# A decoder block with expert retrieval: the second token tile's top-k moved partly into its own rows, thinner top-k pieces beside block 1's attention, and the first tile's final norm later

## The chip, the cores and the metric

The kernel runs on one core of one Trainium2 chip. The metric is the device time of one execution in microseconds (us). The engines are PE (TensorE, matmuls), DVE (VectorE), ACT (ScalarE), POOL (GpSimd) and SP (SyncE); each runs its own instruction stream in order, and the streams meet only in semaphores. Sixteen DMA engines move data for all of them.

## The reference, cut to what matters

The input is 1024 tokens of width 1024, float32. A mixer is followed by an expert retrieval layer (PEER) and a final norm:

```
h   = x + mixer(rmsnorm(x))            # stick-breaking attention (8 heads x 64) + mLSTM (4 heads x 128), gated, w_out
hn  = rmsnorm(h)
q   = hn @ w_query                     # 8 retrieval heads, two halves each
s1, s2 = scores of the halves against 128 keys each
v1, i1 = top_k(s1, 16);  v2, i2 = top_k(s2, 16)
top_s, top_c = top_k(v1[:, None] + v2[None, :], 16)         # of 256 candidates
e_idx = i1[top_c // 16] * 128 + i2[top_c % 16];  gate = softmax(top_s)
y   = h + sum over 8 heads x 16 experts of gate * gelu(u[e_idx] . hn) * v[e_idx]
out = rmsnorm(y)
```

Each token has experts of its own, so 128 rows of u and v (8 KB together) are fetched per token: 1.07 GB in all.

## The kernel before

**Two streams of work.** The 1024 tokens are 8 tiles (`TT`) of 128, and 4 blocks (`NB`) of two tiles. The mixer and the query scores run by block (`mix(b)` on each engine), the expert rows by tile. Block 0's mixer runs first and alone, up to its first queries (`N_HEAD` steps). After that a loop `for i in range(TT): for p in range(PP)` goes over 64 *pairs* of expert rows per tile, and every engine works in each pair on the tile's rows and then on some steps of a later block's mixer. A *slot* is one pair counted over all tiles: slot 64 is pair 0 of tile 1.

**One pair on each engine.** POOL gathers a row pair for 128 tokens (L926; 128 rows of 8 KB for each of the two) into `rowsb`, a ring of `RS = 8` rows (4 pairs); it waits for `v_done` before it overwrites a place, and for `experts_ready` before each 32 rows. DVE makes the two dot products (`dot`, L1629) and writes `dots`. ACT applies gelu (L1190), multiplies by the gate (L1202) and builds two diagonal matrices (`spread`, L1207). PE adds the two rows through them (`add_rows`, L856, 16 matmuls) into `yacc` and gives the ring's places back. After that each engine does its mixer steps of this slot.

**Order of the mixer steps.** `spread_ticks` places block b's steps on slots with estimated costs per engine (`slot_load`, `load_of`); the list `steps[slot][b]` is the same for all engines. A step with much work is followed by the next only in the next slot. For block 1 the slots 8 to 99 are used: attention steps (`sba`) in slots 22 to 29, the convolutions and the mLSTM projections (`PROJ2`) in 30 to 42, heads, gates and merge (`N_MIX`) in 43 to 73, then `w_out`, the norm and the queries to slot 99. Weights come in units of 512 KB on SP's queue into a ring of `WR = 3`: a unit's place is filled again once PE has used it.

**Top-k.** `top_parts(i, first, 2)` does the top-k of two retrieval heads (a *group*) of tile i on DVE, in 9 pieces (`TOP_EACH`), each ending in a `yield`. The last one raises `experts_ready`. A tile has 4 groups, 36 pieces. `parts_at[i][p]` says how many pieces pair p of tile i does; they stand between the dots and the mixer steps on DVE. In tile 0 they are the three remaining groups of tile 0 itself (its first group runs before the loop) and all four of tile 1, 63 pieces: none in pairs 0 and 1, then one per pair, two in pairs 44, 48, 52, 56 and 60. In tile 1 they are those of tile 2, from pair 26 on. Pieces 1 to 4 work on 128x128 scores (`max`, `max_index`, `match_replace`), 5 to 7 on 128x256 candidates, 8 and 9 on 128x512 (`eq`) in `wide`, the memory of `sc`.

**Gates.** After a group's last piece ACT takes exp of its scores (`gates`, L1185) and DVE makes the softmax (L1614 to L1618). Tile 0 does it by group in pairs 1, 11, 20 and 29 (`GATES_AT`); tile 1 and later ones once, at pair 62 of the tile before. `load_scores(1, g)` on ACT loads tile 1's scores of group g into `sc` at pairs 12, 13, 21 and 30 of tile 0 (`SCORES_AT`).

**End of a tile.** At pair 0 of the next tile DVE adds `yacc` to the residual (`residual`); ACT squares it at pair 3 into the tensor `wide`, which is the same memory as `sc` (`norm`, L1212); DVE scales at pair 5 (`final_norm`, L1651); ACT stores at pair 7 and loads the next residual at pair 20.

Of the kernel before, what the change touches and what calls it, by code (L numbers as in the profile page):

```python
# [19 lines left out]
TT = T // P  # L20
# [24 lines left out]
NT = 2  # L45
# [20 lines left out]
def build(nc, xT, x, vecs, w_feat, w_if, w_tok, w_merge, w_out, w_query, keysT, uv, rows, out):  # L66
    ctx = ExitStack()
    with ctx:
# [316 lines left out]

        cost = [load_of(b) for b in range(NB)]
        TOP_EACH, BLOCK_END = 9, 36
        GATES_AT, SCORES_AT = (1, 11, 20, 29), (12, 13, 21, 30)
        GATES_OF = ((1, 1), (2, 2), (4, 2), (6, 2))
        N_SLOT = TT * PP  # L390
        N_PARTS = 4 * TOP_EACH


        parts_at = [[0] * PP for i in range(TT)]
        for p in range(PP):
            parts_at[0][p] = 0 if p < 2 else 2 if p >= 44 and p % 4 == 0 else 1
            for i in range(1, TT - 1):
                if i % NT == 1:
                    due = p - 25 if p < BLOCK_END else 10 + (p - BLOCK_END + 1) * 13 // 8
                else:  # L400
                    due = (p - 15) * N_PARTS // 42
                parts_at[i][p] = max(0, min(due, N_PARTS)) - sum(parts_at[i][:p])


        def slot_load(s):
            i, p = divmod(s, PP)
            dve_ = 2.6 + PART_DVE * parts_at[i][p]
            if p == 0 and i > 0:
                dve_ += 4.5
            if p == 5 and i > 0:  # L410
                dve_ += 1.5
            return [2.6, dve_, 5.1]

        def spread_ticks(b, lo, hi, each):
            count, placed, k, behind = [0] * N_SLOT, [0] * N_SLOT, 0, [0.0] * 3
            for s in range(lo, hi):
                even = max(behind) <= 0.0
                behind = [max(0.0, q) + r - e for q, r, e in zip(behind, slot_load(s), (min(each, 6.4), each, each))]
                while k < len(cost[b]):
                    small = max(cost[b][k][:2]) < 0.9  # L420
                    if count[s] == (2 if b == 1 else 1) and not small:
                        break
                    after = [q + r for q, r in zip(behind, cost[b][k])]
                    if max(after) > 2.0 and not (even and count[s] == 0):
                        break
                    behind = after
                    count[s] += not small
                    placed[s] += 1
                    k += 1
            return placed, k  # L430
# [5 lines left out]
        for b in range(1, NB):  # L436
            lo = 8 if b == 1 else NT * (b - 1) * PP - PP + BLOCK_END
            hi = NT * b * PP - PP + BLOCK_END
            each = 5.0
            while spread_ticks(b, lo, hi, each)[1] < len(cost[b]):  # L440
                each += 0.02
            slot_of = []
            for s, n in enumerate(spread_ticks(b, lo, hi, each)[0]):
                steps[s][b] = n
                slot_of += [s] * n
            first = len(cost[b]) - N_QRY
            assert slot_of[first + 5] > (NT * b - 1) * PP + 3
            for g in range(4):
                assert sum(parts_at[NT * b - 1][:slot_of[first + 4 * g + 5] % PP + 1]) <= TOP_EACH * g


        with nc.Block() as block:
# [479 lines left out]
            def _(act):  # L932
# [246 lines left out]
                def gates(i, first, count):  # L1179
                    own = slice(TOPK * first, TOPK * (first + count))  # L1180
                    if (i, first) == (0, 0):
                        act.wait_ge(first_ready, 1)
                    else:
                        act.wait_ge(experts_ready, 4 * i + (first + count) // 2)
                    act.activation(gate[:, i % 2, own], gate_raw[:, own], ACT.Exp).then_inc(gexp_done, 1)  # L1185
# [6 lines left out]
                def spread(i, p):  # L1192
                    if i == 0 and p % 16 == 0:
                        act.wait_ge(gate_step, 3 * (p // 16) + (6 if p > 0 else 3))
                    elif i == 0 and p == 8:
                        act.wait_ge(gate_step, 6)
                    elif p == 0:
                        act.wait_ge(gate_step, 3 * i + 15)
                    act.wait_ge(gelu_done, i * PP + p + 1)
                    for k in (2 * p, 2 * p + 1):  # L1200
                        s = k % RS
                        act.activation(wg[:, s:s + 1], gmt[:, s:s + 1], ACT.Copy,  # L1202
                                       scale=gate[:, i % 2, k:k + 1]).then_inc(wg_done, 1)
                    act.wait_ge(wg_done, i * NSEL + 2 * p + 2)
                    for k in (2 * p, 2 * p + 1):
                        s = k % RS
                        last = act.activation(diag[:, s, :], ident7[:, :], ACT.Copy, scale=wg[:, s:s + 1])  # L1207
                    last.then_inc(diag_done, 1)
# [17 lines left out]
                for i in range(TT):  # L1226
                    for p in range(PP):
                        gelu(i, p)
                        spread(i, p)
                        if i > 0 and p == 3:  # L1230
                            norm(i - 1)
                        if p == 7 and i > 0:
                            store_out(i - 1)
                        if p == 20:
                            load_h(i)
                        if i == 0 and p in SCORES_AT:
                            load_scores(1, SCORES_AT.index(p))
                        if i > 0 and i % NT == 0 and p == 12:
                            for g in range(4):
                                load_scores(i + 1, g)  # L1240
                        if i + 1 < TT and p == PP - 8:
                            load_hn(i + 1)
                        for b in range(NB):
                            for _n in range(steps[i * PP + p][b]):
                                next(later[b], None)
                        if i == 0 and p in GATES_AT:
                            gates(0, *GATES_OF[GATES_AT.index(p)])
                        if i + 1 < TT and p == PP - 2:
                            gates(i + 1, 0, PH)
                act.activation(ss7[:, 1:2], eps[:, 0:1], ACT.Sqrt)  # L1250
                for c in range(2):
# [10 lines left out]
            def _(dve):  # L1262
# [344 lines left out]
                    yield  # L1607

                def gates(i, first, count):
                    n = i + 4 if i > 0 else GATES_OF.index((first, count)) + 1 if first > 0 else 0  # L1610
                    heads = slice(first, first + count)
                    g3 = gate[:, i % 2, TOPK * first:TOPK * (first + count)].rearrange("p (h k) -> p h k", k=TOPK)
                    dve.wait_ge(gexp_done, n + 1)
                    dve.tensor_reduce(gs[:, heads], g3, AX.X, ALU.add).then_inc(gate_step, 1)  # L1614
                    dve.wait_ge(gate_step, n * 3 + 1)
                    dve.reciprocal(gs[:, heads], gs[:, heads]).then_inc(gate_step, 1)
                    dve.wait_ge(gate_step, n * 3 + 2)
                    dve.tensor_tensor(g3, g3, gs[:, heads].unsqueeze(2).broadcast_to([P, count, TOPK]),  # L1618
                                      ALU.mult).then_inc(gate_step, 1)
# [39 lines left out]
                for _part in top_parts(0, 1, 1):  # L1659
                    pass  # L1660
                gates(0, 0, 1)
                for i in range(TT):
                    todo = [(0, 2 * g, 2) for g in range(1, 4)] if i == 0 else []
                    todo += [(i + 1, 2 * g, 2) for g in range(4)] if i + 1 < TT else []
                    parts = itertools.chain.from_iterable(top_parts(*each) for each in todo)
                    for p in range(PP):
                        dot(i, 2 * p)
                        dot(i, 2 * p + 1)
                        if i > 0 and p == 0:
                            residual(i - 1)  # L1670
                        for _n in range(parts_at[i][p]):
                            next(parts, None)
                        if i == 0 and p - 1 in GATES_AT:
                            gates(0, *GATES_OF[GATES_AT.index(p - 1)])
                        if i > 0 and p == 5:
                            final_norm(i - 1)
                        for b in range(NB):
                            for _n in range(steps[i * PP + p][b]):
                                next(later[b], None)
                    for _part in parts:  # L1680
                        pass
                    if i + 1 < TT:
                        gates(i + 1, 0, PH)
                residual(TT - 1)
                dve.wait_ge(std7_ready, TT)
# [59 lines left out]
```

## Time and profile before

| | |
|---|---|
| time, median of 3 runs | 3381.67 us (3380.03 to 3387.03) |
| profiled execution: its own time, its span | 3383.8 us, 3382.0 us |
| busy: PE, DVE, ACT, POOL | 2630.2, 2134.6, 1082.6, 1195.0 us |
| DMA | 1280.42 MB, of which 1073.81 MB are expert rows; mean 379 GB/s |
| mean granted TensorE clock | 0.893 of full |

The span runs from the first to the last instruction. In the rows below a busy time is the union of an engine's instructions; the DMA share is the mean busy share of the 16 DMA engines; an idle time in square brackets stands ahead of an instruction and names what ended it.

### The profile page before, as it was taken

The numbers are of one execution on the slowest core, as the hardware profiler recorded it, in microseconds if no ns is written. First come the engines' busy times: TensorE is split into PE (matmuls) and PEld (weight loads), VectorE is DVE, ScalarE is ACT, GpSimd is POOL, SyncE is SP. The second block draws the span as 40 slices with busy tenths as digits, with TensorE's granted clock in tenths as the row PEclk, the third lists the DMA queues.
The fourth block names the chain that finished last, engine by engine and source line by source line (L and its number), as shares of the span: only waits on it lengthen the run. The fifth ranks groups of instructions, "written<-read, shape, count | busy, mean of one in ns | idle before, by whom it ended". The sixth has DMA issues, their size and how long they took to land.

```text
span 3382.0 us, 40413 instructions
## 1 busy us (share of the span) xinstructions
PE 2630.2 (78%) x14560; PEld 1344.7 (40%) x14560; DVE 2134.6 (63%) x4989; ACT 1082.6 (32%) x3404; POOL 1195.0 (35%) x1049
## 2 busy tenths in 40 slices
PE   8998887899898777997778777998886555555555
PEld 5775543465364233653344334454352111111111
DVE  2323668885457888775447898776448756765444
ACT  3111434233223553332323463332322232223222
POOL 0001332333233443343334454343334444444443
PEclk8999998999899999999899999999898887776777
DMA  3346996999999999999999999999999999999997
GB/s 113 112 130 211 416 410 263 342 411 417 416 414 417 417 391 417 418 417 417 418 413 408 411 363 416 418 411 416 419 415 410 417 421 420 418 418 415 421 421 324
DMA packets 226839, 1280.42 MB, mean 379 GB/s; under 512 B 25168, under 2 KB 27216, under 8 KB 95568
## 3 DMA queue, kind: packets, MB, share of 16 engines
q0 software_dynamic: 147456, 1073.81, 77.4%
q1 hardware_dynamic: 64272, 162.09, 13.1%
q10 hardware_dynamic: 14912, 41.95, 3.2%
q8 instruction: 115, 1.88, 0.2%
q14 instruction: 84, 0.69, 0.1%
HBM read 1260.97 MB, written 16.78 MB: 378 GB/s over the span
## 4 chain that ended last, share of the span: by engine, by line
DMA 38%; PE 34%; DVE 13%; issue 6%; ACT 6%; POOL 3%; ACTq 0%; DVEq 0%; POOLq 0%; SPq 0%
DMA rowsb<-uv,e_idx 36%; PE yacc L856 13%; PE mixp L571 9%; DVE rowsb L1629 6%; POOL rowsb L926 3%; PE mixp L622 2%; PE mixp L596 2%; PE mixp L583 2%; DVE area L1297 2%; PE mixp L633 2%; ACT diag L1207 2%; ACT wg L1202 2%; DMA wt<-w_query_ 1%; DMA wt<-w_merge 1%; ACT area L944 1%
## 5 line engine op out<-in xcount | busy, mean ns | idle before, releaser
L926 POOL DMA_INDIRECT rowsb<-uv,e_idx x1024 | 1190.3, 1162 | 2157.2 <-PE yacc L856 1671.6
L1629 DVE CUSTOM_DVE_ANT_0 rowsb<-rowsb,hnrow 128x1024 f32<-128x1024 f32 x1024 | 1240.8, 1223 | 834.9 <-DMA rowsb<-uv,e_idx 820.8
L856 PE MATMUL yacc<-rowsb,diag 64*64 64x512 f32 x8192 | 1223.9, 722 | 676.7 <-ACT diag L1207 665.9
L856 PEld LDWEIGHTS yacc<-rowsb,diag 64*64 64x64 f32 x8192 | 300.7, 151 | 1422.7 <-ACT diag L1207 987.8
L1190 ACT ACTIVATE gmt<-dots 128x2 f32<-128x2 f32 x512 | 104.1, 203 | 1742.7 <-DVE dots L1629 1741.2
L571 PE MATMUL mixp<-area,wt 128*128 128x256 f32 x2304 | 539.4, 389 | 10.2 <-ACT area L944 8.9
L571 PEld LDWEIGHTS mixp<-area,wt 128*128 128x128 f32 x2304 | 435.2, 193 | 147.4 <-issue 91.6
L1207 ACT ACTIVATE diag<-ident,wg 128x64 f32<-128x64 f32 x1024 | 300.3, 340 | 16.7
L944 ACT ACTIVATE area<-mixp 128x512 f32<-128x512 f32 (+3 forms) x384 | 163.4, 467 | 348.8 <-PE mixp L571 213.2
L1202 ACT ACTIVATE wg<-gmt,gate 128x1 f32<-128x1 f32 x1024 | 245.6, 286 | 17.5
L596 PE MATMUL mixp<-area,wt 128*128 128x256 f32 x960 | 224.2, 387 | 9.1 <-DMA wt<-w_query_ 8.6
L596 PEld LDWEIGHTS mixp<-area,wt 128*128 128x128 f32 x960 | 179.0, 191 | 82.9 <-issue 40.6
L633 PE MATMUL mixp<-area,wt 128*128 128x256 f32 x512 | 118.9, 386 | 4.7 <-DMA wt<-w_merge 4.7
L622 PE MATMUL mixp<-wt,area 128*128 128x512 f32 x256 | 117.6, 607 | 0.0
L583 PE MATMUL mixp<-wt,area 128*128 128x512 f32 x256 | 116.7, 602 | 0.0
L633 PEld LDWEIGHTS mixp<-area,wt 128*128 128x128 f32 x512 | 96.2, 192 | 33.0 <-issue 13.9
L1297 DVE TENSOR_TENSOR_SCAN area<-area 128x128 f32<-128x128 f32 (+7 forms) x64 | 87.0, 1359 | 2.2
L1629 DVE DVE_READ_ACCUMULATOR2_ANT dots<- 128x1 f32 x1024 | 84.2, 82 | 0.0
L622 PEld LDWEIGHTS mixp<-wt,area 128*128 128x128 f32 x256 | 47.4, 193 | 72.3 <-issue 71.4
L583 PEld LDWEIGHTS mixp<-wt,area 128*128 128x128 f32 x256 | 46.8, 190 | 70.5 <-issue 70.4
L1190 ACT ACT_TABLE_LOAD x46 | 59.0, 1283 | 0.8
L670 PE MATMUL mixp<-keys_sb,area 64*128 64x512 f32 (+3 forms) x192 | 50.2, 587 | 11.0 <-ACT area L944 8.6
(200 smaller groups left out, 1707.0 us busy)
## 6 DMA issues: line engine op xcount, KB each, us to landing
wt<-w_merge SPq DMA_DIRECT2D x96, 512.0 KB
wt<-w_feat SPq DMA_DIRECT2D x80, 512.0 KB
wt<-w_query_ SPq DMA_DIRECT2D x64, 512.0 KB
wt<-w_tok SPq DMA_DIRECT2D x32, 512.0 KB
wt<-w_out_ SPq DMA_DIRECT2D x32, 512.0 KB
rowsb<-uv,e_idx POOLq DMA_INDIRECT x1024
area<-x_rows ACTq DMA_DIRECT2D x4, 1024.0 KB
area<-keysT ACTq DMA_DIRECT2D x16, 256.0 KB
```

The lines of the kernel that those rows point to most:

```text
L571: last = pe.matmul(X[:, bank(key), at:at + N], w[:, c * P:(c + 1) * P], src[:, c, :], start=c == 0, stop=c == KD - 1)
L583: last = pe.matmul(X[:, bank(key), :], xn[:, 2 * n + c, t * P:(t + 1) * P], w[:, c * NCH:(c + 1) * NCH], start=n == 0 and c == 0, stop=n = ...
L596: last = pe.matmul(X[:, bank(key), at:at + N], w[:, c * NCH + f * P:c * NCH + (f + 1) * P], hnT[:, 2 * m + c, :], start=m == 0 and c == 0 ...
L622: last = pe.matmul(X[:, bank(key), :], mgT[:, n, t * P:(t + 1) * P], w[:, c * NCH:(c + 1) * NCH], start=n == 0, stop=n == KD - 1)
L633: last = pe.matmul(X[:, bank(key), f * N:(f + 1) * N], w[:, at:at + P], src[:, c, :], start=c == 0, stop=c == 3)
L856: last = pe.matmul(yacc[at:at + HP, k % 2, c * NCH:(c + 1) * NCH], diag[r * HP:(r + 1) * HP, s, :], rowsb[r * HP:(r + 1) * HP, s, D + c * ...
L926: pool.indirect_dma_start(rowsb[:, n % RS, :], None, uv, bass.IndirectOffsetOnAxis(ap=e_idx[:, i % 2, k:k + 1], axis=0)).then_inc(row_load ...
L944: act.activation(to, src, fn, **kw).then_inc(x_taken[bank(key)], 1)
L1190: act.activation(gmt[:, s:s + 2], dots[:, s:s + 2], ACT.Gelu).then_inc(gelu_done, 1)
L1202: act.activation(wg[:, s:s + 1], gmt[:, s:s + 1], ACT.Copy, scale=gate[:, i % 2, k:k + 1]).then_inc(wg_done, 1)
L1207: last = act.activation(diag[:, s, :], ident7[:, :], ACT.Copy, scale=wg[:, s:s + 1])
L1629: dve.tensor_tensor_reduce(rowsb[:, s, 0:D], rowsb[:, s, 0:D], hnrow[:, i % 2, :], 1.0, 0.0, ALU.mult, ALU.add, dots[:, s:s + 1]).then_inc ...
```

## The change

- `parts_at`: the pieces of tile 0 and tile 1 become one list over slots (`todo`). Slots 2 to 19 do one piece each (18 pieces, tile 0's second and third groups). Slots 20 to 39 do 9 pieces (slots 22, 24, 26, 28, 31, 33, 35, 37, 39: tile 0's fourth group). Slots 40 to 82 do the 36 pieces of tile 1, so 20 of them fall in tile 0 and 16 in pairs 1 to 18 of tile 1.
- `GATES`: tile 0's last gates at slot 40 instead of 29; tile 1's gates by group at slots 62, 65, 74 and 84 instead of all at slot 62. `spread` in tile 1 waits by group. `load_scores(1, 3)` moves from pair 30 to 41.
- ACT's `norm(0)` moves from pair 3 of tile 1 to pair 19, behind a wait for `experts_ready` 8, since it overwrites `sc`; `final_norm(0)` from pair 5 to 21, `store_out(0)` from 7 to 23, `load_h(1)` from 20 to 36. Later tiles stay as they are.
- The planner's allowance for PE becomes `max(6.4, each - 1.0)` per slot. With the new `slot_load` of DVE, block 1's steps stay in slots 8 to 98: the attention steps end in slot 30 instead of 29, `PROJ2` and the first `N_MIX` steps lie one slot later, from slot 60 on the steps lie one slot earlier. Blocks 2 and 3 keep their slots.

```diff
-        GATES_AT, SCORES_AT = (1, 11, 20, 29), (12, 13, 21, 30)
-        GATES_OF = ((1, 1), (2, 2), (4, 2), (6, 2))
+        SCORES_AT = (12, 13, 21, 41)
+        GATES = ((1, 0, 1, 1), (11, 0, 2, 2), (20, 0, 4, 2), (40, 0, 6, 2),
+                 (62, 1, 0, 2), (65, 1, 2, 2), (74, 1, 4, 2), (84, 1, 6, 2))
+        GATES_AT = {slot: n for n, (slot, i, first, count) in enumerate(GATES)}
...
-            parts_at[0][p] = 0 if p < 2 else 2 if p >= 44 and p % 4 == 0 else 1
...
+        for n in range(83):
+            i, p = divmod(n, PP)
+            if n < 20:
+                parts_at[i][p] = 1 if n >= 2 else 0
+            elif n < 40:
+                parts_at[i][p] = (n - 19) * TOP_EACH // 20 - (n - 20) * TOP_EACH // 20
+            else:
+                parts_at[i][p] = (n - 39) * N_PARTS // 43 - (n - 40) * N_PARTS // 43
...
-                behind = [max(0.0, q) + r - e for q, r, e in zip(behind, slot_load(s), (min(each, 6.4), each, each))]
+                behind = [max(0.0, q) + r - e for q, r, e in zip(behind, slot_load(s), (min(each, max(6.4, each - 1.0)), each, each))]
...
-                        if i > 0 and p == 3:
+                        if i == 1 and p == 19:
+                            act.wait_ge(experts_ready, 8)
+                        if i > 0 and p == (19 if i == 1 else 3):
                             norm(i - 1)
-                        if p == 7 and i > 0:
+                        if i > 0 and p == (23 if i == 1 else 7):
                             store_out(i - 1)
-                        if p == 20:
+                        if p == (36 if i == 1 else 20):
                             load_h(i)
...
+                todo = [(0, 2 * g, 2) for g in range(1, 4)] + [(i, 2 * g, 2) for i in range(1, TT) for g in range(4)]
+                parts = itertools.chain.from_iterable(top_parts(*each) for each in todo)
                 for i in range(TT):
-                    todo = [(0, 2 * g, 2) for g in range(1, 4)] if i == 0 else []
-                    todo += [(i + 1, 2 * g, 2) for g in range(4)] if i + 1 < TT else []
-                    parts = itertools.chain.from_iterable(top_parts(*each) for each in todo)
...
-                        if i > 0 and p == 5:
+                        if i * PP + p - 1 in GATES_AT:
+                            gates(*GATES[GATES_AT[i * PP + p - 1]][1:])
+                        if i > 0 and p == (21 if i == 1 else 5):
                             final_norm(i - 1)
```

## Rows read from the trace of the kernel before

**Rows 1.** The page: the span in 40 slices of 84.55 us, three of its lines
```profile
DVE  2323668885457888775447898776448756765444
...
DMA  3346996999999999999999999999999999999997
GB/s 113 112 130 211 416 410 263 342 411 417 416 414 417 417 391 417 418 417 417 418 413 408 411 363 416 418 411 416 419 415 410 417 421 420 418 418 415 421 421 324
```

**Rows 2.** Busy time by stage: stretch, length, busy (instructions), granted clock, DMA share, GB/s
```profile
340.00:500.00 160.00, 138.52 (x750) 78.38 (x749) 96.25 (x269) 58.19 (x165) 52.15 (x46) 0.94 1.02 416
500.00:560.00 60.00, 40.20 (x295) 18.95 (x297) 56.34 (x125) 32.90 (x90) 14.37 (x12) 0.85 0.67 247
560.00:640.00 80.00, 66.04 (x332) 36.04 (x324) 69.47 (x196) 23.20 (x67) 26.30 (x22) 0.92 0.85 324
640.00:700.00 60.00, 57.60 (x305) 32.98 (x308) 42.72 (x130) 20.99 (x61) 20.41 (x19) 0.94 0.96 372
700.00:780.00 80.00, 80.00 (x477) 52.16 (x470) 65.12 (x178) 34.24 (x95) 29.69 (x28) 1.00 1.02 418
780.00:920.00 140.00, 116.38 (x573) 59.98 (x575) 69.98 (x126) 38.54 (x122) 41.86 (x39) 0.93 1.02 416
```

**Rows 3.** DVE's timeline: first dots of pairs 25, 26, and pair 25's piece
```profile
505.21 1.22 DVE L1629 CUSTOM_DVE_ANT_0 rowsb<-rowsb,hnrow 128x1024 f32<-128x1024 f32 x1
...
507.50 0.08 DVE L1570 MATCH_VALUE_LOAD topi<-top,sc 128x8 f32 x1
...
509.08 0.28 DVE L1294 TENSOR_TENSOR area<-area,tri 128x128 f32<-128x128 f32 x1
...
512.65 1.22 DVE L1629 CUSTOM_DVE_ANT_0 rowsb<-rowsb,hnrow 128x1024 f32<-128x1024 f32 x1
```

**Rows 4.** DVE busy on `sc` alone, in pairs 23 to 30 and 32 to 39
```profile
488.05:555.75 67.70, 13.14 (x51) 0.85 0.74 280
567.42:630.91 63.49, 13.14 (x51) 0.92 0.87 332
```

**Rows 5.** Waits of 488 to 556 us: total, times, longest
```profile
POOL rowsb L926 <- PE yacc L856: 46.7, 7, 11.2
...
DVE area L1294 <- ACT area L1031: 2.0, 1, 2.0
...
DVE gs L1614 <- ACT gate L1185: 1.2, 1, 1.2
```

**Rows 6.** The chain that ended last, around pairs 29 to 31
```profile
545.77 3.62 PE yacc L856 x16
...
553.65 1.28 ACT L1185
...
555.20 1.28 ACT L1190
...
557.88 3.69 PE yacc L856 x16
561.57 4.25 PE mixp L716 x16
```

**Rows 7.** PE's timeline beside `PROJ2`, in slots 34 to 40
```profile
588.18 3.69 PE L856 MATMUL yacc<-rowsb,diag 64*64 64x512 f32 x16 [4.38 <-ACT diag L1207]
591.80 4.58 PE L571 MATMUL mixp<-area,wt 128*128 128x256 f32 x16
...
612.35 1.95 PE L856 MATMUL yacc<-rowsb,diag 64*64 64x512 f32 x16 [2.58 <-ACT diag L1207]
614.22 3.72 PE L571 MATMUL mixp<-area,wt 128*128 128x256 f32 x16
620.32 3.20 PE L856 MATMUL yacc<-rowsb,diag 64*64 64x512 f32 x16 [2.37 <-ACT diag L1207]
```

**Rows 8.** Waits in 780 to 920 us, all engines
```profile
ACT gmt L1190 <- DVE dots L1629: 89.0, 16, 15.1
...
DVE rowsb L1629 <- DMA rowsb<-uv,e_idx: 30.2, 17, 2.5
DVE area L1480 <- PE mixp L633: 19.0, 4, 8.1
```

**Rows 9.** The chain around 840 us: a weight unit's landing
```profile
829.72 16.70 DMA wt<-w_merge
```

**Rows 10.** ACT's timeline at tile 0's final norm
```profile
803.15 1.04 ACT L1212 ACTIVATE sc<-acc 128x1024 f32<-128x1024 f32 x1
...
804.30 1.28 ACT L1214 ACT_TABLE_LOAD   x1
```

**Rows 11.** DVE's scaling of the final norm, the group of the whole run
```profile
L1651 DVE SCALAR_TENSOR_TENSOR acc<-acc,ss,fnorm 128x1024 f32<-128x1024 f32 x7 | 9.0, 1285 | 0.3
```

More of the change, by code:

```diff
@@ L448, in build @@
             for g in range(4):
-                assert sum(parts_at[NT * b - 1][:slot_of[first + 4 * g + 5] % PP + 1]) <= TOP_EACH * g
+                assert sum(parts_at[NT * b - 1][20:slot_of[first + 4 * g + 5] % PP + 1]) <= TOP_EACH * g
         with nc.Block() as block:
@@ L1196, in spread @@
                         act.wait_ge(gate_step, 6)
-                    elif p == 0:
-                        act.wait_ge(gate_step, 3 * i + 15)
+                    elif i == 1 and p % 16 == 0:
+                        act.wait_ge(gate_step, 3 * (p // 16) + 18)
+                    elif i > 1 and p == 0:
+                        act.wait_ge(gate_step, 3 * i + 24)
                     act.wait_ge(gelu_done, i * PP + p + 1)
@@ L1245, in _ @@
                                 next(later[b], None)
-                        if i == 0 and p in GATES_AT:
-                            gates(0, *GATES_OF[GATES_AT.index(p)])
-                        if i + 1 < TT and p == PP - 2:
+                        if i * PP + p in GATES_AT:
+                            gates(*GATES[GATES_AT[i * PP + p]][1:])
+                        if 1 < i + 1 < TT and p == PP - 2:
                             gates(i + 1, 0, PH)
@@ L1609, in gates @@
                 def gates(i, first, count):
-                    n = i + 4 if i > 0 else GATES_OF.index((first, count)) + 1 if first > 0 else 0
+                    n = i + 7 if i > 1 else 0 if (i, first) == (0, 0) else [g[1:3] for g in GATES].index((i, first)) + 1
                     heads = slice(first, first + count)
@@ L1672, in _ @@
                             next(parts, None)
-                        if i == 0 and p - 1 in GATES_AT:
-                            gates(0, *GATES_OF[GATES_AT.index(p - 1)])
-                        if i > 0 and p == 5:
+                        if i * PP + p - 1 in GATES_AT:
+                            gates(*GATES[GATES_AT[i * PP + p - 1]][1:])
+                        if i > 0 and p == (21 if i == 1 else 5):
                             final_norm(i - 1)
@@ L1679, in _ @@
                                 next(later[b], None)
-                    for _part in parts:
-                        pass
-                    if i + 1 < TT:
+                    if 1 < i + 1 < TT:
                         gates(i + 1, 0, PH)
```

## The prediction

> **What bounds the kernel.** I read the page's slices first, then busy time by stage, then the chain of waits. From slice 6 on the DMA line is all nines and the rate about 418 GB/s, except in the slices with 263 and 342 GB/s, two shallower dips, and the tail [rows 1]. So the kernel is bound by the bytes of the rows, and it loses time only where the DMA engines lie idle. The stages give the first hole a size [rows 2]: against 418 GB/s, 500 to 560 us at 247 lose 60 x 171/418 = 24.5 us, 560 to 640 at 324 lose 18.0, 640 to 700 at 372 lose 6.6: 49 us together. The reader is to see two things in these lines. In the first two DVE is busy 56.3 of 60 and 69.5 of 80 us. In the third PE is, 57.6 of 60, and then 80.0 of 80 up to 780 us. So DVE is the bound from about 488 to 631 us (pairs 23 to 39), and PE from there to the end of tile 0. After 700 us the DMA is full again.
>
> What DVE does in this time is dots, a top-k piece and attention or convolution, one after another without idle time: pair 25 lasts from 505.21 to 512.65, of which 507.50 to 509.08 is the piece [rows 3]. The rows for later pairs have landed long before; POOL waits 46.7 us for PE to give places back [rows 5]. A microsecond taken from DVE there is one that the DMA idles less, and as the DMA is full afterwards and to the end, nothing later gives it back.
>
> **The change, part by part.**
>
> *Pieces out of the attention.* On `sc`, DVE is busy 13.14 us in pairs 23 to 30 and 13.14 us in 32 to 39, 8 pieces each: 1.64 us a piece, from both rows [rows 4]. In the first stretch 3 pieces stay of 8 (slots 24, 26, 28), so 5 x 1.64 = 8.2 us go. In the second 4 stay of 8 (33, 35, 37, 39), so 4 x 1.64 = 6.6 us go. Gross: 14.8 us. The pieces in between and behind (31, 40 to 63) I take at nothing: pair 31 waits for PE, and from slot 40 on PE is the bound [rows 2].
>
> *What the waits take back.* At pair 23 DVE already waits 2.0 us for ACT behind its piece [rows 5]; with no piece it waits longer, so 1.1 us of a thin piece are not gained. Around pairs 29 to 31 the chain leaves DVE and goes over PE and ACT [rows 6], and a piece taken off there (pairs 29, 30) may bring nothing: bounds 0 and 2 x 1.64 = 3.3 us lost, I take 2.0. Beside `PROJ2` there is a loop: diag of pair p, 16 matmuls into `yacc`, 16 of the unit, and the convolution of pair p+1 waits for these. PE waits for diag there 4.4, 2.6, 2.4 us [rows 7], so it has about 2 us of slack in a pair and seldom becomes the bound if a pair shortens by 1.64; bounds 0 and all 6.6, I take 1.5.
>
> *Clock.* In this stretch the granted clock is 0.92, and 1.00 in 700 to 780 us [rows 2]. Behind the gap of 4.38 us the 16 matmuls take 3.69 us and the unit 4.58, against 1.95 and 3.72 elsewhere [rows 7], so at the lower level of 1.2 GHz; at 620 us 3.20 against 1.95. With shorter gaps some of these (1.74 + 0.86 + 1.25 = 3.9 us) come back: bounds 0 and 3.9, I take 2.1. The Trainium skill, TensorE: Matmul & The Clock Gate, Part 1, states that the throttled clock is the default and that activity releases it. By that rule the whole 3.9 us would come back and the time would be 1.8 us lower; the gap of 4.38 us and the slow matmuls behind it agree.
>
> *Gates of tile 0 at slot 40.* The exp and gelu tables, 1.28 us each, now lie on the chain in pair 30 [rows 6]. At slot 40 PE runs without gaps and has just got ahead; I take half of the 2.6 us as paid again there: a gain of 1.3 (bounds 0 and 2.6).
>
> *The 16 pieces in tile 1's pairs 1 to 18.* They cost 16 x 1.64 = 26.2 us of DVE in a stretch where DVE is busy 70.0 of 140 us and the DMA is full at 416 GB/s [rows 2]. What hides them is the DMA: DVE itself waits 30.2 us for rows [rows 8]. If that cover were gone they would cost up to 26.2 us. I take 0. Of the gates by group the same holds: three more times two table loads, 6 x 1.28 = 7.7 us on ACT, which is busy 38.5 of 140 us there and waits 89.0 us for dots [rows 2, 8].
>
> *The later norm.* It costs what it cost: 1.04 us of ACT and a table load of 1.28 [rows 10], 1.3 us of DVE [rows 11], 16 pairs later. The new wait for `experts_ready` 8 stands behind `spread` of slot 83, which needs DVE's dots of slot 83, and these stand behind the last piece in slot 82: it is always met. Queued behind it on ACT are gelu of pair 20 and the steps of block 1's queries, whose scores enter `sc` in slot 87, after the norm. SP and POOL wait for none of these; `load_h(1)` at pair 36 has 28 pairs until it is read. The two DMAs on ACT's queue (512 KB each) move within a full stretch. Cost 0; if ACT's 2.3 us should meet a critical gelu, 2.3.
>
> *Planner.* `PROJ2` one slot later and the last heads one slot earlier move one unit into tile 0: 3.7 us of PE [rows 7] in a stretch where PE and DMA are both full, against the same less in tile 1. Taken as 0, bounds -3.7 and +3.7.
>
> Sum: 14.8 - 1.1 - 2.0 - 1.5 + 2.1 + 1.3 = 13.6 us. To this comes a little for tile 0's pairs 44 to 47, where two pieces stood in pair 44 and DVE's dots came late for a PE that is idle 2.4 us of 60 [rows 2]: bounds 0 and 2.4, I take 1.0. That makes 14.6 us off the span of 3382.0 (own time 3383.8; the median of the runs shown, 3381.67, is 2.1 below it and within their spread). From the median: 3367.
>
> **The rivals.**
>
> *All of the hole closes (much faster).* For it: in tile 1 pairs with queries and pieces run with a full DMA. If the pieces that went were what made the chain switch between DVE, ACT and PE, then the gross 14.8 + 2.6 + 3.9 and the 6.6 us of 640 to 700 us come: 27.9, so 3354, and with part of the attention's remaining hole 3345. Against it: without a piece an attention pair is 7.44 - 1.58 = 5.9 us [rows 3], against 5.0 us that two rows of 1.05 MB take at 418 GB/s, and PE's stretch to 780 us is not touched.
>
> *The next engine takes over (no change).* PE and ACT need in a pair almost what DVE does: the loop over diag and the unit has 2 us of slack [rows 7]. And a fuller DMA makes weights late: a unit of w_merge took 16.70 us to land at a full DMA [rows 9]; a unit is asked for three pairs ahead, less the 3.7 us of its own matmuls, so at 16.7 us a pair can't be shorter than (16.7 + 3.7)/3 = 6.8 us. The second stretch has 7.9 us a pair now (63.49/8) and 7.1 after 6.6 us less: just above. Should units take 20 us, the second stretch gains nothing, and with the first stretch's deductions 3 to 6 us are left: 3377. The Trainium skill, DMA: Bandwidth & Descriptors, Issuing engines are not separate DMA queues, states that transfers of all issuing engines run on the same 16 DMA engines and interleave; the 16.70 us agree with it. By that rule each row pair that comes earlier delays a unit, and the 3377 of this case is where it would lead.
>
> *Tile 1 pays (slower).* The mechanism: in slots 65 to 82 DVE runs the merge steps in order, and it already waits 19.0 us for PE's `bml` units there [rows 8], with PE waiting for weights. A piece ahead of each step delays the merge, so PE, so the ring of 8 rows, whose turn from landing to the next gather has 20 us of DMA work less the turn itself. It decides if the DMA share of 780 to 920 us falls under 1.0; with all 26.2 us paid, the time is 3367 + 26 = 3393. Against it: 70.0 + 26.2 = 96 of 140 us leaves DVE far from full [rows 2], and most of its wait is for data, under which the piece hides.
>
> **Chances.** Forecast case (8 to 24 us off) 0.60; all of the hole 0.15; the next engine takes over 0.17; tile 1 pays 0.08. Range: to the slow side up to the takeover's 3377 and half the clock's term, 3379; to the fast side into the first rival, 3350. Outside lie the slower case and the far end of the faster one, 0.17 to 0.2. A change under 0.2% (6.8 us) can't be told from none here: faster 0.77, same 0.16, slower 0.07.
>
> **What would show it.** In the profile after: the two low slices rise (263 to about 300, 342 to about 370 GB/s); 500 to 560 us carries more than 247 GB/s; pairs 23 to 39 take some 130 us from the first attention dots instead of 143, and DVE's waits between its dots grow there; tile 1 begins 14 to 15 us sooner; 780 to 920 us stays at 416 GB/s with DVE busy near 96 us. Wrong it would be if PE's waits for diag vanish while the pairs keep their length (takeover), or if the DMA share behind tile 0 falls under 1.0 (tile 1 pays), or if the weights' landing stands on the chain before 700 us.

## The result, and the profile after

The changed kernel takes 3363.84 us (median of 4, 3361.08 to 3369.19) against 3384.35 us for the kernel before (median of 4, 3380.03 to 3388.74). The ratio is 0.994, 95% interval 0.9927 to 0.9952: 20.5 us faster by the medians. The forecast was 3367 in 3350 to 3379. A second comparison (a0 below) gave 0.9948.

The profiled execution is the slowest of its four, 3369.19 us with a span of 3367.4. So its rows show 14.6 of the 20 us. A second trace of the same kernel (a0 below) has a span 22.7 us under that of the kernel before.

The page after, the two lines of the DMA in the 40 slices (84.2 us each), against [rows 1]:

```profile
DMA  3346998999999999999999999999999999999997
GB/s 113 113 129 211 416 410 322 373 408 402 416 416 418 419 392 417 414 417 417 418 416 414 404 363 410 418 418 416 418 415 408 417 419 421 418 417 410 421 421 326
```

The slices with 263 and 342 GB/s now have 322 and 373. The dips of 392 and 363, where blocks 2 and 3 have their attention, and the tail of 326 stand as they were.

Busy time by stage, for the same stretches as [rows 2] (stretch, length, busy of PE, PEld, DVE, ACT, POOL with instructions, granted clock, DMA share, GB/s):

```profile
340.00:500.00 160.00, 136.02 (x746) 75.71 (x744) 93.15 (x257) 58.86 (x168) 50.09 (x46) 0.95 1.02 415
500.00:560.00 60.00, 48.86 (x355) 23.21 (x356) 53.08 (x101) 30.58 (x92) 24.78 (x17) 0.89 0.83 307
560.00:640.00 80.00, 66.62 (x341) 34.71 (x343) 69.51 (x189) 29.98 (x85) 25.49 (x24) 0.96 0.94 363
640.00:700.00 60.00, 60.00 (x341) 38.49 (x329) 39.18 (x108) 20.36 (x60) 18.20 (x17) 0.94 0.99 384
700.00:780.00 80.00, 78.76 (x456) 52.15 (x453) 61.86 (x167) 33.61 (x89) 29.98 (x24) 1.00 1.00 409
780.00:920.00 140.00, 118.66 (x598) 59.96 (x600) 89.63 (x221) 45.22 (x133) 50.08 (x44) 0.94 1.01 411
```

The same sum as in the prediction, what the DMA moved less than 418 GB/s: 60 x 111/418 = 15.9 us, then 10.5, 4.9, 1.7 and 2.3, together 35.3 us. Before it was 24.5 + 18.0 + 6.6 + 0 + 0.7 = 49.8. The difference is 14.5 us; the spans differ by 14.6. Both kernels move the same bytes, so this sum says where the gain lies, in 500 to 700 us, and that nothing behind 920 us gives it back; which part of the change made it, it doesn't say.

How long DVE's stretches are. DVE's timeline after: the first attention instruction of pair 23 with the wait ahead of it, and the first dots of pairs 31 and 41:

```profile
492.71 0.29 DVE L1307 TENSOR_TENSOR area<-area,tri 128x128 f32<-128x128 f32 x1 [3.06 <-ACT area L1040]
...
543.39 1.22 DVE L1642 CUSTOM_DVE_ANT_0 rowsb<-rowsb,hnrow 128x1024 f32<-128x1024 f32 x1
...
616.15 1.22 DVE L1642 CUSTOM_DVE_ANT_0 rowsb<-rowsb,hnrow 128x1024 f32<-128x1024 f32 x1
```

And DVE's busy time on `sc` in pairs 23 to 30 and in pairs 33 to 40, which now do the convolution steps that 32 to 39 did, against [rows 4]:

```profile
487.27:543.39 56.12, 3.13 (x20) 0.85 0.86 325
556.98:616.15 59.17, 7.42 (x20) 0.94 0.91 347
```

Pairs 23 to 30 take 56.12 us instead of 67.70. The top-k there fell from 13.14 to 3.13 us, by 10.0 us, and the gates went too: all of it came through. The wait of 2.0 us for ACT in pair 23 grew to 3.06, by the piece that went, as forecast. The convolution pairs take 59.17 instead of 63.49 us while their top-k fell by 5.7 us: 4.3 came through.

All of pairs 23 to 39 take 123.3 us (487.27 to the first dots of pair 40 at 610.55) instead of 142.9; the forecast said some 130. But one convolution step now stands behind them, in pair 40, and pairs 40 to 63, where PE is busy 60.00 of 60 us in 640 to 700, take 155.2 us instead of 146.1. So 9 of these 19.6 us are spent again before tile 1 begins. No weight unit stands on the chain that ended last between 480 and 700 us, the third sign of being wrong that the prediction named.

### The profile page after: what moved, and what is told of

Read it like the earlier page. It is cut to its first block, busy times and chain, and to the rows that moved or that the text cites. A ratio compares the mean times of both kernels' runs of the same rounds, so it can differ in the third digit from the quotient of the medians.

```text
span 3367.4 us, 40433 instructions
## 1 busy us (share of the span) xinstructions
PE 2634.3 (78%) x14560; PEld 1337.6 (40%) x14560; DVE 2134.9 (63%) x4998; ACT 1087.6 (32%) x3411; POOL 1192.8 (35%) x1049
## 4 chain that ended last, share of the span: by engine, by line
DMA 40%; PE 33%; DVE 12%; issue 6%; ACT 5%; POOL 3%; ACTq 0%; POOLq 0%; DVEq 0%; SPq 0%
DMA rowsb<-uv,e_idx 39%; PE yacc L865 13%; PE mixp L580 8%; DVE rowsb L1642 6%; POOL rowsb L935 3%; PE mixp L592 2%; PE mixp L605 2%; DVE area L1310 2%; ACT diag L1218 2%; PE mixp L631 2%; ACT wg L1213 2%; PE mixp L642 2%; DMA wt<-w_query_ 1%; ACT gmt L1199 1%; ACT area L953 1%
## 5 line engine op out<-in xcount | busy, mean ns | idle before, releaser
L865 PE MATMUL yacc<-rowsb,diag 64*64 64x512 f32 x8192 | 1236.4, 729 | 666.5 <-ACT diag L1218 655.9
L1218 ACT ACTIVATE diag<-ident,wg 128x64 f32<-128x64 f32 x1024 | 300.3, 340 | 16.7
L679 PE MATMUL mixp<-keys_sb,area 64*128 64x512 f32 (+3 forms) x192 | 54.2, 630 | 10.6 <-ACT area L953 8.0
## 6 DMA issues: line engine op xcount, KB each, us to landing
area<-keysT ACTq DMA_DIRECT2D x16, 256.0 KB, 11.5
```

Of the source, the lines that this page charges most:

```text
L865: last = pe.matmul(yacc[at:at + HP, k % 2, c * NCH:(c + 1) * NCH], diag[r * HP:(r + 1) * HP, s, :], rowsb[r * HP:(r + 1) * HP, s, D + c * ...
```

## The experiments

Every kernel was timed against the kernel before, whose median was 3385.0 us beside a0 to a3, 3386.9 beside b1 to b4, 3385.9 beside c1 to c3 and 3387.5 beside d1. So a kernel's gain is read against the kernel before of its own comparison: by the medians the changed kernel is 20.5 us faster in the first and 20.1 in a0. The intervals of the ratios reach some 3 to 5 us to either side, and a smaller difference between two kernels is not shown by them. Line numbers of `DVE` and `ACT` differ a little from kernel to kernel.

### a0: the changed kernel again

No edit.

> The changed kernel once more, for the size of the change beside its parts. The times so far gave 20 us off; the profiled executions differ by 14.6 us of span. If the DMA's idle time in tile 0 is the whole effect, the median lies 14 to 21 us under the kernel before, ratio 0.994 to 0.996.

Measured: 3364.86 us, ratio 0.9948 (0.9936 to 0.996). Its profiled execution has a span of 3359.3 us. Its first dots of tile 1, and those of the first trace (DVE's timelines of a0 and of the changed kernel before it):

```profile
756.74 1.15 DVE L1642 CUSTOM_DVE_ANT_0 rowsb<-rowsb,hnrow 128x1024 f32<-128x1024 f32 x1
```
```profile
765.74 1.15 DVE L1642 CUSTOM_DVE_ANT_0 rowsb<-rowsb,hnrow 128x1024 f32<-128x1024 f32 x1
```

One program, 9.0 us apart at the start of tile 1 and 8.1 in the span. In 640 to 700 us, where PE is the bound, the granted clock is 1.00 in a0 and 0.94 in the first trace, so some of its matmuls ran at the lower level. A difference of some us between two single traces of this kernel says nothing; the medians over several executions do.

### a1 and a2: the pieces alone, the planner alone

a1 is the change with block 1's steps in their old slots, a2 the kernel before with the steps in the new ones (`new_parts` is the new table):

```diff
 # a1, on the changed kernel
-            dve_ = 2.6 + PART_DVE * parts_at[i][p]
+            dve_ = 2.6 + PART_DVE * old_parts[i][p]
-                ... (min(each, max(6.4, each - 1.0)), each, each))]
+                ... (min(each, 6.4), each, each))]
 # a2, on the kernel before
-            dve_ = 2.6 + PART_DVE * parts_at[i][p]
+            dve_ = 2.6 + PART_DVE * new_parts[i][p]
-                ... (min(each, 6.4), each, each))]
+                ... (min(each, max(6.4, each - 1.0)), each, each))]
```

> All of the change but the planner: block 1's steps stand in the slots of the kernel before (the planner counts with the old pieces and the old PE allowance). Theory: the gain is DVE work taken out of pairs 23 to 39, so nearly all of it is here, 12 to 20 us off, and DVE's stretch from the first attention dots to the last convolution is 10 to 15 us shorter than before. Rival 1 (the steps' new slots make the gain): under 5 us off.

> Only the planner's part of the change: block 1's steps in the new slots, the pieces, gates and norm as before. Theory: within 5 us of the kernel before, as the same work stands in one pair more or less and DVE stays the bound from pair 23 to 40. Rival 1: 10 us or more off.

Measured: a1 3365.2 us, 0.9946 (0.9933 to 0.9958), the same as all of the change. Its pairs 23 to 39 hold the same mixer steps as those of the kernel before, so they are the cleanest measure of the pieces and the gates. DVE on `sc` in them:

```profile
484.24:610.61 126.37, 12.03 (x43) 0.92 0.87 334
```

They take 126.4 us against 142.9 (488.05 to 630.91), 16.5 us less, for 15.1 us of top-k (27.15 before, 12.03 now) and the gates that went. Expected were 10 to 15. a2 3379.68 us, 0.9981 (0.9973 to 0.999): 5 us by the medians, 6 by the ratio, so at the edge of what was expected, and far from the 20. The two don't add: with the pieces gone, the new slots bring nothing that can be measured. Rival 1 fell.

### a3: only the gates of tile 0's last group at slot 40

```diff
-        GATES_AT, SCORES_AT = (1, 11, 20, 29), (12, 13, 21, 30)
+        GATES_AT, SCORES_AT = (1, 11, 20, 40), (12, 13, 21, 30)
```

> The kernel before with tile 0's last gates (exp, its two table loads, softmax on DVE) at slot 40 instead of 29, nothing else. Theory: at most 2.6 us off, since the tables come back at slot 40; forecast 1.3. Rival 2 (the switch of the chain from DVE to ACT in pair 30 is the large cost): 5 us or more off.

Measured: 3379.91 us, 0.9986 (0.9977 to 0.9994), about 5 us (2 to 8 by the interval), against 1.3 forecast. That is where rival 2 said 5 us or more; the interval still reaches down to the theory's 2.6. Where the time goes, PE's timeline shows; first the kernel before, in pairs 29, 30 and 31, then a3:

```profile
545.77 3.62 PE L856 MATMUL yacc<-rowsb,diag 64*64 64x512 f32 x16 [3.04 <-ACT diag L1207]
557.88 3.69 PE L856 MATMUL yacc<-rowsb,diag 64*64 64x512 f32 x16 [4.55 <-ACT diag L1207]
```
```profile
543.42 3.10 PE L856 MATMUL yacc<-rowsb,diag 64*64 64x512 f32 x16 [2.72 <-ACT diag L1207]
552.56 1.95 PE L856 MATMUL yacc<-rowsb,diag 64*64 64x512 f32 x16 [1.59 <-ACT diag L1207]
```

The two table loads (1.28 us each) hold ACT ahead of the diagonal, PE's gap becomes 4.55 us, and the 16 matmuls behind it take 3.69 us instead of 1.95. DVE then waits for the `if` matmuls; its wait for them in the two traces (the kernel before, then a3):

```profile
DVE area L1347 <- PE mixp L716: 6.9, 1, 6.9
```
```profile
DVE area L1347 <- PE mixp L716: 3.4, 1, 3.4
```

3.5 us less, and the 1.2 us wait for the gate [rows 5] is gone. Pairs 30 and 31 together take 16.8 us in the kernel before (550.60 to 567.42), 16.7 in the trace of c3 (below), which has the loads there too, and 11.5 in a3's (548.24 to 559.70). In a3 the loads stand at 626.69 and 628.23, where pairs 40 to 43 take 15.3 us against 14.8. So the loads were worth more than their length in pairs 30 and 31, and no more than 0.5 us was paid again in pairs 40 to 43.

How much of this is PE's clock is open. The 16 matmuls and the 16 of `if` behind them take 2.4 us longer in the kernel before than in a3, and behind a gap of 4.55 us the first 16 were slow in both traces that have it (3.69 us in c3's too). But behind the short gap of 1.59 us they ran at the lower level in 4 of the 12 traces that have it (the changed kernel, b2, b3, d1). The first trace of the changed kernel:

```profile
548.18 3.60 PE L865 MATMUL yacc<-rowsb,diag 64*64 64x512 f32 x16 [1.59 <-ACT diag L1218]
```

### b1 and b2: the load given back

b1 puts two max instructions into the five attention pairs that lost a piece, b2 into four pairs beside the convolutions. Their result is used by nothing.

```diff
                         for _n in range(parts_at[i][p]):
                             next(parts, None)
+                        if i == 0 and p in (23, 25, 27, 29, 30):          # b2: (32, 34, 36, 38)
+                            dve.max(spare[:, 0, :], hnrow[:, i % 2, :])
+                            dve.max(spare[:, 1, :], hnrow[:, i % 2, 0:256])
```

> The changed kernel with idle work given back to DVE: in the five pairs of the attention that lost a piece (23, 25, 27, 29, 30) two max instructions over 1024 and 256 elements of hnrow, some 1.6 us a pair (an estimate from the 0.28 us of a max over 128 and the 0.42 us over 256). Theory: DVE is the bound there, so most of the 8 us comes back: 4 to 8 us over the changed kernel, that is ratio 0.9960 to 0.9972. Rival (the chain over ACT and PE hides it): within 2 us of the changed kernel.

> The same load in four pairs beside the convolutions that lost a piece (32, 34, 36, 38), 6.5 us of DVE. Theory: 4 to 6 us come back, ratio 0.9960 to 0.9966. Rival (PE and the weights bound these pairs already, so that the pieces taken out there brought nothing): within 2 us of the changed kernel.

Measured: b1 3369.9 us, 0.9958 (0.9944 to 0.9972); b2 3369.48 us, 0.9955 (0.9942 to 0.9969); both ratios just under the bands that were expected. Against the kernel before of their comparison they are 17.0 and 17.4 us faster, some 3 us less than the changed kernel's 20.5 and 20.1; the intervals overlap, so by the times alone neither cost is shown. The lengths of the stretches are the sharper measure. DVE on `spare` in pairs 23 to 30 of b1, and in pairs 32 to 40 of b2:

```profile
484.58:546.53 61.95, 7.75 (x10) 0.86 0.86 326
```
```profile
549.14:620.43 71.29, 6.20 (x8) 0.89 0.88 340
```

b1's stretch is 61.95 us against 56.12 of the changed kernel: 7.75 us of load make it 5.8 longer, and the part of pair 23 went into the wait there. The 56.12 hold in a0's trace too (56.14), and in b2's, so the 5.8 us are clear of what single traces differ by. b2's is 71.29 against 68.98 (547.17 to 616.15): 6.20 us of load make it 2.3 longer. But the same stretch takes 65.3 us in a0's trace (545.13 to 610.44) and 65.0 in b1's, and against these it would be 6 us. So DVE is the bound in the attention; beside the convolutions it is at least in part, and how far one trace of b2 can't tell.

### b3: 22 us more DVE in tile 1's first pairs

```diff
+                        if i == 1 and 1 <= p <= 18:
+                            dve.max(spare[:, p % 2, :], hnrow[:, i % 2, :])
```

> The changed kernel with one max over 1024 elements of hnrow in each of the pairs 1 to 18 of tile 1, 18 x 1.2 = 22 us more DVE (estimate) where the moved pieces stand. Theory: the full DMA hides it, within 3 us of the changed kernel. Rival (the pieces moved there are paid in part, the DMA was at 411 instead of 416 GB/s in 780 to 920 us): 8 us or more over it.

Measured: 3363.46 us, 0.9938 (0.9925 to 0.9952). The stage view of b3:

```profile
780.00:920.00 140.00, 121.37 (x620) 63.63 (x620) 106.69 (x227) 46.28 (x135) 48.42 (x42) 0.94 1.02 416
```

DVE is busy 106.7 of 140 us, 70.0 before the change, and the DMA stays at 416 GB/s. By the medians b3 is 23.4 us faster than the kernel before, so no cost of the moved pieces shows, nor of 22 us more. The 411 GB/s of the first trace are not seen here, nor are the rival's 8 us.

### b4, c1 and c2: other places for tile 0's last group

b4 does its 9 pieces in slots 31 to 39. c1 does all of tile 0's 27 pieces in slots 2 to 22 and keeps the steps of the changed kernel; c2 is c1 with the planner run anew.

```diff
 # b4
-                parts_at[i][p] = (n - 19) * TOP_EACH // 20 - (n - 20) * TOP_EACH // 20
+                parts_at[i][p] = 1 if n >= 31 else 0
 # c1, c2
-            if n < 20:
-                parts_at[i][p] = 1 if n >= 2 else 0
+            if n < 23:
+                parts_at[i][p] = 0 if n < 2 else 2 if n in (14, 15, 18, 20, 21, 22) else 1
             elif n < 40:
-                parts_at[i][p] = (n - 19) * TOP_EACH // 20 - (n - 20) * TOP_EACH // 20
+                parts_at[i][p] = 0
```

> The changed kernel with tile 0's last group done one piece per pair in slots 31 to 39, none in 20 to 30. The planner places the steps anew. Theory: the attention's stretch gets 3 x 1.64 = 4.9 us shorter in DVE and the convolutions' 4 to 5 pieces longer, so about even, within 3 us of the changed kernel. Rival (a piece beside the convolutions is free since PE bounds them): 4 us or more below it.

> The changed kernel with the last group of tile 0 finished before the attention: slots 2 to 22 do 27 pieces (two in 14, 15, 18, 20, 21 and 22), slots 23 to 40 none; block 1's steps kept in the slots of the changed kernel. In the changed kernel's trace DVE waits 3.6, 4.7 and 9.2 us in pairs 20, 21 and 22 with the DMA full, so pieces there are hidden. Theory: 8 more pieces, 13 us, leave DVE's stretch; by the price that the two loads showed (some 5 us of time for 6.5 to 8 us of DVE), 6 to 9 us below the changed kernel, ratio 0.992 to 0.993. Rival (next engine): within 3 us of it.

> The same pieces with the planner run anew on them. Its attention and convolution steps stay in the same slots, some later heads move by one. Theory: within 2 us of c1. Rival (slots of the steps matter as much as the pieces): 4 us or more apart from it.

Measured: b4 3367.67 us, 0.9953 (0.9939 to 0.9966), 19.2 us faster by the medians, so as the changed kernel within the noise and without the rival's 4 us. (b2's ratio is 0.9955: one such comparison doesn't tell the two apart.) c1 3355.99 us, 0.9909 (0.9892 to 0.9925); c2 3356.49 us, 0.9915 (0.99 to 0.993), as c1. c1 is 29.9 us faster than the kernel before, so 9 to 10 us more than the changed kernel, a little over the 6 to 9 of the theory, and its interval lies apart from those of both comparisons of the changed kernel (0.9927 to 0.9952, 0.9936 to 0.996). The stage view of c1, and DVE on `sc` in its attention pairs:

```profile
340.00:500.00 160.00, 134.66 (x765) 75.51 (x765) 107.25 (x299) 61.14 (x173) 51.65 (x47) 0.97 1.02 417
500.00:560.00 60.00, 47.08 (x374) 25.17 (x368) 51.79 (x91) 34.08 (x95) 26.99 (x20) 1.00 0.91 334
560.00:640.00 80.00, 68.75 (x357) 36.34 (x358) 61.78 (x168) 28.04 (x81) 25.52 (x24) 0.98 0.98 390
```
```profile
484.83:538.67 53.84, 0.00 (x0) 0.94 0.94 358
```

DVE has 14.1 us more to do in 340 to 500 us and the DMA runs at 417 GB/s there as before. With no piece at all the eight attention pairs still take 53.84 us, 6.7 a pair, and carry 358 GB/s, and DVE is busy for 49.33 of the 53.84 us; so the rest of the hole is for the most part the attention's own scans and dots. The clock of 500 to 560 us is 1.00 now.

### c3: only the late norm

```diff
-                        if i > 0 and p == 3:
+                        if i > 0 and p == (19 if i == 1 else 3):
                             norm(i - 1)
 # and final_norm(0) at 21, store_out(0) at 23, load_h(1) at 36, as in the change
```

> The kernel before with tile 0's norm at pair 19 of tile 1, its scaling at 21, store at 23 and the next residual's load at 36, nothing else. Theory: no change, ratio 0.999 to 1.001, as the DMA is full there. Rival (the norm's table loads sat on the chain in pair 3): 0.998 or less.

Measured: 3388.05 us, 1.0013 (1.0003 to 1.0022). No gain is in it; there may be a cost of some 4 us, just outside what was expected. The profiled executions don't show it (span 3380.7 against 3382.0), and I have no cause for it.

### d1: 18 us more DVE where PE is the bound

```diff
+                        if i == 0 and 44 <= p <= 61 and parts_at[i][p]:
+                            after_marks()
+                            mark7(dve.max(spare[:, p % 2, :], hnrow[:, i % 2, :]))
```

> The changed kernel with one max over 1024 elements of hnrow (1.22 us, as the earlier loads measured) in each of the 15 pairs with a piece from 44 to 61 of tile 0, 18 us more DVE. Theory (PE is the bound there, so that pieces cost nothing in these pairs): within 3 us of the changed kernel, ratio 0.994 to 0.9955. Rival (the pieces of these pairs cost as much as those beside the attention, 0.6 to 0.8 us of time for each us of DVE): 10 us or more over it, ratio 0.997 or more.

Measured: 3370.36 us, 0.9952 (0.9939 to 0.9966). The ratio is in the theory's band, and the interval lies under the rival's 0.997. By the medians it is 17.1 us faster than the kernel before of its comparison, some 3 us less than the changed kernel, for 18.4 us of load; that is within the noise. So DVE work in pairs 44 to 61 is cheap, but I can't call it free.

## Why the prediction was right, point by point

- **The bound.** Right. The DMA's idle time fell by 14.5 us and the span by 14.6, and nothing behind 920 us gave it back. "Nothing later gives it back" is too strong for tile 0 itself: pairs 40 to 63 took 9.1 us longer in the same trace, in part because a convolution step moved there from pair 39.
- **Pieces out of the attention.** Right in kind, too small in size. The forecast took 5 x 1.64 = 8.2 us and gave back 1.1 and 2.0. Measured were 10.0 us of top-k gone, because the three pieces that stayed are thin ones (the mean of 1.64 was the wrong price for them), and all of it came through. The 2.0 us for pairs 29 and 30 were not lost: with the table loads out of pair 30 as well, the chain stays on DVE.
- **Gates of tile 0 at slot 40.** The term most off: 1.3 us forecast, about 5 alone (a3, 2 to 8 by the interval). The step that failed was "I take half of the 2.6 us as paid again there", and the bounds of 0 and 2.6, which left out that ACT's delay makes the `if` matmuls late for DVE: its wait for them fell from 6.9 to 3.4 us, on top of some 1.8 us in pair 30.
- **Beside the convolutions.** 6.6 - 1.5 + 2.1 = 7.2 us forecast, 4.3 measured. The gross was 5.7 and not 6.6, since the four pieces that stay (6 to 9) are the thick ones: 7.42 us. Against 5.7 the 1.4 that did not come through are near the deduction of 1.5, and the 2.1 of the clock don't show in this trace. In a0's the stretch takes 57.1 us (553.33 to 610.44), 6.4 less than before. The clock rose from 0.92 to 0.96 in 560 to 640 us (0.98 in a0's); how much that brought by itself was not measured. Nor was the 1.0 us for pairs 44 to 47.
- **Pieces in tile 1's pairs.** Cost 0, right, and b3 shows it with a second load. DVE was busy 89.6 us in 780 to 920 us, against the forecast's 96.
- **Pieces of pairs 40 to 63.** Taken at nothing, right as far as d1 can show: some 3 us for 18.4 us of DVE, within the noise.
- **Planner.** Taken at 0 on top of the pieces, and a1 agrees. Alone (a2) it is worth 5 to 6 us (3 to 9 by the interval), so probably more than the bound of 3.7, which was worked out for one unit and not for attention steps spread over one more pair.
- **The late norm.** Taken at 0; c3 has it between 0.03% and 0.22% slower.
- **The rivals.** The slices rose as said (322 and 373 against about 300 and 370). The takeover by the next engine can be no more than the 1.4 us of 5.7 that did not come through beside the convolutions in the first trace, and did not decide. Tile 1 did not pay. The hole did not close: 35 of 50 us are left. Tile 1 began 11.3 us sooner in the first trace and 20.3 in a0's, around the 14 to 15 forecast.

Two errors met: the attention with its gates brought about 5 us more, the convolutions 3 us less. The sum of 14.6 is that of the first trace by luck as much as by its terms; the medians say 20, and a0's trace 22.7.

## What to carry to other kernels

Where a full DMA is the bound, look for its few low slices, and ask which engine is busy in them and where nearby the same engine waits for data: work moved from the first place to the second is gained nearly whole (c1: 10.6 us more of top-k moved, 9 to 10 gained by the medians), and in the second no cost showed here. Price the pieces that stay and those that go one by one, since a mean over thin and thick ones is off by a fifth here. A small delay on a side engine inside the loop (two table loads) is to be priced with what waits behind it: here 2.6 us of loads were worth some 5.

## What the runs showed that I had not expected

Two table loads of 1.28 us ahead of one diagonal were worth some 5 us of the kernel's time (a3). PE's gap in front of the matmuls is 4.55 us with them and 1.59 without. The same 16 matmuls take 3.69 us behind the long gap in both traces that have it; behind the short one they take 1.95 us in 8 traces and 3.55 to 3.64 in 4. The Trainium skill, TensorE: Matmul & The Clock Gate, Part 1, states that activity releases a clock that is throttled by default. The long gap agrees with it; the four slow groups behind 1.59 us show that this gap alone does not decide the clock.

One program's executions spread over 8 to 14 us (a0: 3361.07 to 3374.75), and two traces of it differ in the granted clock of the stretch in which PE is the bound, 0.94 and 1.00.
